# Forgetting attention of a two-group decoder step: another block order, one turning of the gate rows, other places for the chains at block ends

## The reference, cut to what matters

```
cum = jnp.cumsum(logf, axis=1)                      # one gate row per head
s = einsum('bqhe,bkhe->bhqk', q, k) * SCALE         # prompt: 2048 x 2048, causal
s = s + cum[query] - cum[key]
out = einsum('bhqk,bkhe->bqhe', softmax(s), v)
```

## Time and profile before

| | |
|---|---|
| three runs | 3190.3, 3173.29, 3172.47 us (median 3173.29) |
| the profiled execution's own time | 3176.38 us |
| its span | 3174.6 us |
| PE, DVE, ACT, POOL busy in the span | 93%, 51%, 31%, 24% |
| granted TensorE clock, mean of the span | 0.97 |

### The profile page before, as it was taken

One profiled execution on the slowest core, in us unless ns is written; L12 is line 12 of the kernel. 1 busy time (PEld: TensorE's weight loads), 2 busy tenths in 40 slices (PEclk: granted clock), 3 DMA queues, 4 the chain that ended last, 5 costly groups with the idle time before them and its releaser, 6 DMA issues. The chain is left out here.

```text
span 3174.6 us, 44387 instructions
## 1 busy us (share of the span) xinstructions
PE 2963.3 (93%) x15753; PEld 2460.9 (78%) x15753; DVE 1629.9 (51%) x3067; ACT 976.5 (31%) x2022; POOL 747.1 (24%) x510
## 2 busy tenths in 40 slices
PE   8999999878877899979979999999999999999998
PEld 6888889744344499967769999999998788888886
DVE  5113210367677688865745555554556544444445
ACT  4223221355555455543232221112214111111112
POOL 4002100123433254532101122211121221122210
PEclk9999999888999899989989999999999999999999
DMA  4465336456665334337653111112113411111101
GB/s 155 157 212 175 112 130 177 145 151 197 174 185 164 95 112 113 97 95 243 197 195 138 40 40 40 40 43 77 40 47 109 151 53 40 40 40 60 59 13 54
DMA packets 237238, 349.80 MB, mean 110 GB/s; under 512 B 75321, under 2 KB 172122, under 8 KB 231119
## 3 DMA queue, kind: packets, MB, share of 16 engines
q1 hardware_dynamic: 236151, 325.40, 32.7%
q0 software_dynamic: 944, 22.61, 1.9%
HBM read 283.14 MB, written 93.97 MB: 119 GB/s over the span
## 5 line engine op out<-in xcount | busy, mean ns | idle before, releaser
L2706 POOL TENSOR_TENSOR cm_dn_lo<-cm_dn_raw,cm_dn_hi 128x1024 fp32r<-128x1024 f32 x44 | 108.3, 2482 | 974.4 <-ACT cm_dn_hi L2755 974.4
L3443 PE MATMUL pj_acc<-pj_w_hi,pj_h_hi 128*128 128x480 f32 (+3 forms) x896 | 335.1, 374 | 0.9 <-DVE pj_h_lo L3318 0.9
L3444 PE MATMUL pj_acc<-pj_w_lo,pj_h_hi 128*128 128x480 f32 (+3 forms) x896 | 333.5, 372 | 0.0
L3445 PE MATMUL pj_acc<-pj_w_hi,pj_h_lo 128*128 128x480 f32 (+3 forms) x896 | 333.3, 372 | 0.0
L2999 PE MATMUL cm_g_ps<-cm_h_hi,cm_up_hi 128*128 128x344 f32 (+1 forms) x880 | 310.4, 353 | 12.0 <-DVE cm_h_lo L2811 10.9
L3001 PE MATMUL cm_g_ps<-cm_h_hi,cm_up_lo 128*128 128x344 f32 (+1 forms) x880 | 309.0, 351 | 0.0
L2999 PE MATMUL cm_u_ps<-cm_h_hi,cm_up_hi 128*128 128x344 f32 (+1 forms) x880 | 308.2, 350 | 0.0
L3000 PE MATMUL cm_g_ps<-cm_h_lo,cm_up_hi 128*128 128x344 f32 (+1 forms) x880 | 308.2, 350 | 0.0
L3001 PE MATMUL cm_u_ps<-cm_h_hi,cm_up_lo 128*128 128x344 f32 (+1 forms) x880 | 307.8, 350 | 0.0
L3000 PE MATMUL cm_u_ps<-cm_h_lo,cm_up_hi 128*128 128x344 f32 (+1 forms) x880 | 307.0, 349 | 0.0
L3324 DVE TENSOR_TENSOR pj_w_lo<-area,pj_w_hi 128x480 fp32r<-128x480 f32 (+3 forms) x112 | 75.6, 698 | 381.2 <-ACT pj_w_hi L3280 381.1
(11 more groups left out here) (459 smaller groups left out, 6557.7 us busy)
## 6 DMA issues: line engine op xcount, KB each, us to landing
area<-in_w_up SPq DMA_DIRECT2D x44, 1024.0 KB, 6.8
fp_kv_low<-in_fox_kv SPq DMA_DIRECT2D x168, 256.0 KB, 2.9
area<-in_fox_kv SPq DMA_DIRECT2D x88, 256.0 KB, 2.9
cm_dn_raw<-in_w_down SPq DMA_DIRECT2D x44, 512.0 KB, 3.6
out_s_win<-in_cache POOLq DMA_DIRECT2D x8, 2047.0 KB, 9.2
proj_a<-area SPq DMA_DIRECT2D x48, 240.0 KB
sp_raw<-proj_b SPq DMA_DIRECT2D x16, 640.0 KB, 4.2
area<-in_w_a SPq DMA_DIRECT2D x10, 960.0 KB, 7.0
```

The costliest lines, as they stand in the source:

```text
L2706: pool.tensor_tensor(dn_lo[:, s], dn_raw[:, s], dn_hi[:, s].bitcast(F32), ALU.subtract).then_inc(dn_ready, 1)
L3443: pe.matmul(out, h_hi[:, k, place(t)], w_hi[:, j % 2, k, 0:wide], start=(k == 0), stop=False)
L3444: pe.matmul(out, h_hi[:, k, place(t)], w_lo[:, j % 2, k, 0:wide], start=False, stop=False)
L3445: last = pe.matmul(out, h_lo[:, k, place(t)], w_hi[:, j % 2, k, 0:wide], start=False, stop=(k == KT - 1))
```

## The change

- **Order of blocks.** Heads 1 and 3 take their blocks in falling order, so the blocks have 4, 8, 12, 16, 16, 12, 8, 4, 4, 8, 12, 16, 16, 12, 8, 4 slots. The scores of the next block are spread evenly over 3 or 4, 7, 10 or 14 slots of a block of 4, 8, 12 or 16.
- **Gate rows.** `k_aug` keeps the rows of all heads side by side, so one turning gives 16 rows; the gate parts are 4 and no longer 16. POOL copies them once to the second half of `k_more`. `m_tok` and the rows of `q_more` have 16 rows too, zero outside the head's own four.
- **Places.** Query parts come in slot 1, keys in slots listed in `keys_at`. At a block's end PE does `turn_max` and then the block's last `value` (the other way round after blocks of 4 slots); `copy_o` comes ahead of the next block's first `exp`.
- **Output.** The turning of the output is a matmul with `fold`, two unit matrices one above the other, which adds the halves; `normalise` is one instruction, from one buffer `o_tok`. Blocks of 4 slots get one more small matmul, with zeros, that clears a corner of `o_ps`.
- **Sample.** `attend` does the 16 pages of a part in its slot 15, the four groups are fetched again from slot 16 on, the result is kept at slot 17, and `product` is two POOL instructions of half the size.
- **Start.** The fill of `q_more` goes from POOL to DVE in the projection; the first scores come after four of the first six parts.

```diff
-    blocks = [(h, q) for h in range(H) for q in range(4)]
+    blocks = [(h, q if h % 2 == 0 else 3 - q) for h in range(H) for q in range(4)]
...
+    scores_at = {}
+    for b in range(NBLK - 1):
+        within = {4: 4 if size[b + 1] == 8 else 3, 8: 7, 12: 10, 16: 14}[size[b]]
+        for n in range(size[b + 1]):
+            scores_at.setdefault((b, n * within // size[b + 1]), []).append(n)
+
+    keys_at = {(0, 3): (0, 2), (1, 5): (0, 3),
+               (2, 5): (1, 0), (2, 7): (1, 1), (2, 9): (1, 2), (3, 5): (1, 3),
+               (5, 5): (2, 0), (5, 7): (2, 1), (5, 9): (2, 2), (6, 5): (2, 3),
+               (9, 5): (3, 0), (10, 5): (3, 1), (10, 7): (3, 2), (10, 9): (3, 3)}
+    parts_at = {at: [("k", *part)] for at, part in keys_at.items()}
+    parts_at[0, 0], parts_at[1, 6] = [("a", 2)], [("a", 3)]
+    for b in range(NBLK - 2):
+        parts_at[b, 1] = [("q", b + 2)]
...
-                            fetched < RING or part_slot((fetched - RING) // QUARTS, 16 + (fetched - RING) % QUARTS) <= slot):
+                            fetched < RING or part_slot((fetched - RING) // QUARTS, 16) <= slot):
...
-                pool.tensor_tensor(prod[:, n % 2], quarter(n)[:, :, 0],
-                                   q_own[:, a // 2:a // 2 + 1].to_broadcast([P, QUART, F]), ALU.mult
-                                   ).then_inc(multiplied, 1)
+                for pair in (slice(0, 2), slice(2, 4)):
+                    last = pool.tensor_tensor(prod[:, n % 2, pair], quarter(n)[:, pair, 0],
+                                              q_own[:, a // 2:a // 2 + 1].to_broadcast([P, 2, F]), ALU.mult)
+                last.then_inc(multiplied, 1)
...
-                    if at == 20:
+                    if at == 17:
                         keep(a)
...
-                    if at in range(15, 15 + QUARTS):
-                        attend(a, at - 15)
+                    if at == 15:
+                        for k in range(QUARTS):
+                            attend(a, k)
...
+                    if b == 2 and i == 0:
+                        pool.wait_ge(part_hi, part_no["a", 3])
+                        pool.tensor_copy(k_more[0:AUGS, 1], k_more[0:AUGS, 0].bitcast(F32)).then_inc(aug_spread, 1)
...
             def normalise(b):
...
-                dve.link(v, v.tensor_copy(o[:, j:], z[:, j:, 0]))
-                v.tensor_tensor(o[:, j:], o[:, j:], z[:, j:, 1], ALU.add).then_inc(o_joined, 1)
-                v.wait_ge(o_joined, b + 1)
-                v.tensor_tensor(o, o, rden[:, b % 2].unsqueeze(2).to_broadcast([P, 4, HD]),
-                                ALU.mult).then_inc(o_ready, 1)
+                if b >= 1:
+                    v.wait_ge(stored[(b - 1) % 2], 16 * ((b - 1) // 2 + 1))
+                v.tensor_tensor(o_tok[:], z_ps[:, 0:4 * HD].rearrange("p (j e) -> p j e", e=HD),
+                                rden[:, b % 2].unsqueeze(2).to_broadcast([P, 4, HD]), ALU.mult).then_inc(o_ready, 1)
...
-                    if i == 2 and b > 0:
+                    if i == 0 and b > 0:
                         copy_o(b - 1)
...
+                    if q == 0 and i == 1:
+                        pe.wait_ge(k_zeroed, 3)
+                        pe.matmul(o_ps[HD:P, 0:P], nothing[:], probs[:, u % PROBS, 0:P], start=True, stop=True)
...
-                    last = pe.transpose(z_ps[:, j * P:(j + 1) * P], oT[:, j * P:(j + 1) * P], ident)
+                    last = pe.matmul(z_ps[:, j * HD:(j + 1) * HD], oT[:, j * P:(j + 1) * P], fold[:], start=True, stop=True)
...
-                    if i == 1 and b > 0:
-                        value(b - 1, size[b - 1] // GROUP - 1)
...
-                if b + 1 < NBLK:
+                if b + 1 < NBLK and size[b] > 4:
                     turn_max(b + 1)
-            value(NBLK - 1, size[NBLK - 1] // GROUP - 1)
+                value(b, size[b] // GROUP - 1)
+                if b + 1 < NBLK and size[b] == 4:
+                    turn_max(b + 1)
```

171 lines of the change are left out of this document (89 added, 82 removed).

## The result

The changed kernel takes 3160.79 us (median of 5 runs, 3154.71 to 3161.12), the kernel before 3180.58 us (median of 5 runs beside them, 3172.47 to 3190.3). The ratio is 0.9935, with a 95% interval of 0.9909 to 0.996: 0.65% faster, some 20 us. The forecast was 3118 us, 55 us less than before; the range began above at 3158. The direction was right, the size a third of what was forecast.

A forecast was written before the change was run, and what follows sets the result against it. The prediction saw a 478.6 us stage with PE standing 108 us, mainly for ACT's score buffers. Terms summed to −54.9 us: 3176.4 became 3121.5, adjusted to 3118 for the runs' median; range 3080 to 3158.

The forecast's parts named there:

- burst and hops: Sample: four `attend` groups at once outlast the two score buffers, +6 us; hops over DVE and PE come closer, +5 us.
- block ends: At block ends, PE's waits for the query split, maxima and row copies all go: −22.2 us, between −25 and −11.
- the edges: Stage start and end: earlier scores without waiting for POOL's fill, −1.5 us; fewer DVE instructions before the last sums, −2.2 us.
- Gate rows: 12 of 16 gate parts go: −7.8 us of PE work and −5.0 us of waits ahead of them.
- taken at the same: Output: `turn_o` as a matmul with `fold` could cost 6 to 23 us; taken as unchanged from 11.5, nothing gained.
- Spreading: Scores spread over slots: one-score slots take 2.05 us, within 1.93 to 2.35; −25.4 us, between −36 and 0.
- third rival: Sample's chain on PE: uncovered bursts and hops cost 6.5 us per part, 104 us in all; 3212 us, chance 0.09.
- Split product: POOL's sample `product` in halves: DVE stands behind POOL half as long, −3 us, between 0 and −8.
- first rival: Dense round stays the bound: one-score slots cost 2.35 us, half of block-end waits return; 3155 us, chance 0.20.
- fourth rival: On SP, a store behind the 16 page issues makes `normalise` hold up DVE: +28 us, 3146 us, chance 0.08.
- second rival: All PE waits in the stage go and the granted clock rises: −97 us, 3076 us, chance 0.13.
- signs given for right and wrong: Right: one-score slots at 2.0 to 2.1 us; wrong: 2.3 us, DVE store waits, or PE waits at 634, 637 or burst.

The follow-up runs named there:

- w1: Changed kernel with rising block order, scores two to a slot as before and key parts in scoreless slots of 16-slot blocks: 3177.06 us, ratio 0.9998 to before.
- v2: Block order, score spreading and key places undone as in w1, plus `attend` and fetches spread and `keep` at slot 20: 3163.05 us, 0.9951 to before.
- x1: Changed kernel with `attend` spread over slots 15 to 18, pages fetched one by one, result kept at slot 20: 3143.89 us, 0.9888 to before.
- v1: Kernel before with only the change's block ends; artefact: its query load kept its old place and came late, 19.1 us. 3204.11 us, 1.0077 to before.
- y2: Changed kernel with `turn_max`, last `value` and `copy_o` in the old order, query parts still in slot 1: 3177.5 us, 0.9989 to before.
- z3: Changed kernel with query parts, and the next head's query load, back to two slots before a block's end: 3168.14 us, 0.9966 to before.
- y3: Changed kernel with the output turned by transposes and its halves joined on DVE as before: 3161.15 us, 0.9938 to before.
- z1: Changed kernel without the 12 key parts and key loads of heads 1 to 3: 3126.64 us, 0.9851 to before.
- z2: Kernel before without the key parts and key loads of heads 1 to 3: 3162.39 us, 0.9956 to before.
- w2: Kernel before with only POOL's `product` split into two half-size instructions: 3173.06 us, 0.9994 to before.
- y4: Changed kernel with `attend` spread as in x1 and key parts moved off `value` slots as in x2: 3134.83 us, 0.9877 to before.
- x4: Changed kernel with scores packed two to a slot from slot 0 of each block: 3194.91 us, 1.0045 to before.
- y1: Changed kernel with every head's blocks in rising order and key parts set anew: 3199.69 us, 1.0056 to before.
- x3: Changed kernel with POOL's `product` as one whole instruction again: 3176.51 us, 0.9985 to before.
- x2: Changed kernel with key parts moved one slot later, off slots with a `value`: 3154.6 us, 0.992 to before.

## Why the prediction was wrong

The direction was right, the size was not: its −55 us were −20. By three pieces, each measured one with about 9 us of uncertainty:

| piece | forecast | measured |
|---|---|---|
| order, spreading, keys (w1 to changed, v2 to x1) | −25 | −20 |
| burst and hops (changed to x1, w1 to v2) | +11 | +15 |
| all the rest (v2) | −40.5 | −16 |
| sum | −55 | −21 |

Most of what is missing lies in the last piece. In v2's stage the terms of that piece forecast 33.9 us less standing of PE (22.2 at block ends, 5.0 at gate parts, 3.0 for the product, 3.7 at the edges) and 6.6 us less work; measured were 12.5 and 0.6 us.

**Block ends: the step that failed.** "All of 13.5 + 5.0 + 3.7 = 22.2 us goes" was read off the list of waits as if each named wait stood by itself. Some of what was named did go: of the 13.5 us for the query's split 0.8 are left, at line 940. But in the changed kernel `turn_max` still stands 14.6 us: 6.6 for the split of a key part and 8.0 for the maxima. Three of the four waits for a key part are at the ends of blocks of 12 slots, where the change puts one in slot 9. With order, scores and key parts as before, in v2, `turn_max` stands only 3.8 us, and what went turns up elsewhere: 7.0 us at `part` and 2.3 at `turn_o`, where query and key parts follow each other through the one bank, and 7.5 us more at `score` (59.5 for 52.0). In v1 `score` stands 11.4 us more. A query part in slot 1 puts two copies on ACT and a split on DVE where the next block's scores begin. The forecast asked what is late next for the last `value` only, not for the place to which the part was moved. All the same y2 and z3, 17 and 10 us slower, show that in the changed kernel the new places are the better ones; its slot 1 has two scores in 6 blocks of 14, that of w1 in 11. What the term is worth by itself is not shown: v1 has the artefact. That it is the copies in slot 1 that delay the scores is read from the lists; no kernel moved them alone onto an engine that is free.

**Gate rows.** The busy part was right: 7.5 us of PE fell away for 7.8 forecast. In v2's stage PE's busy time is unchanged all the same: the gate parts cost 1.2 us there, but the folding matmul 21.3 for 11.5 and the zeros 2.5. `turn_o` had been taken at the same although its upper bound was 11.5 us more; in the changed kernel it came out in the middle. Together with DVE's 15 us, booked at nothing, it makes no difference in time that y3 could show: two errors that cancel, which is luck.

**Spreading.** The one-score slot was taken at 2.05 us. A block of 16 slots with 12 such slots and 4 without scores would by the forecast take 12 × 2.05 + 4 × 1.47 = 30.5 us; the one at 757.94 took 29.39, at a granted clock of 1.00. But it is the best of the four. Its twin at 978.51 took 35.09, and 4.9 of the 5.7 us between them are PE's busy time at a granted clock of 0.85. For the blocks at 936.38 and 715.28 the forecast's values give 2 × 3.22 + 12 × 2.05 + 2 × 1.47 = 34.0 us, and they took 42.13 and 42.66 (715.28 to 757.94); two bursts each lie in them, and granted clocks of 0.84 and 0.92. The forecast's 129 us for the four were 149. So 2.05 us holds for one block at full clock; by the same sum the other three have one-score slots of 2.4 to 2.8 us. The 20 us that the bundle is worth contain, by the medians of z1 and z2, about 13 us lost to key parts. Moving them from slots where ACT and DVE had nothing to do to slots where they hold up a score was a moved step for which the sum had no term.

**The burst.** The place was named and the mechanism was right: it outlasts the two buffers and ACT and DVE run dry. Size: 15 us, with the 11 booked inside its uncertainty; the third rival's 104 us were far off. 0.9 us a part is far below the 4.1 us from which that rival would have decided.

**Split product.** The rule cited in the forecast, from the Trainium skill, SBUF — State Buffer, Who interferes with whom, would make the gain nil if the second half follows at once. The halves do follow at once, and this is what DVE does beside such a pair (changed kernel, POOL and DVE in order of time):

```profile
954.05 2.50 POOL L469 TENSOR_TENSOR fp_prod<-fp_kv_low,fp_q_own 128x512 f32<-128x512 f32 x2 [2.85 <-DVE fp_s_dec L514]
...
954.48 0.87 DVE L547 TENSOR_SCALAR fp_p_row<-fp_extra,sp_consts 8x4 f32<-8x4 f32 x1
955.27 0.20 DVE L549 TENSOR_REDUCE fp_den_dec<-fp_p_dec 128x4 f32<-128x64 f32 x1
955.50 1.06 DVE L550 TENSOR_TENSOR fp_den_dec<-fp_den_dec,fp_extra 1x4 f32<-1x4 f32 x1
```

DVE's first instruction ends at 955.35, where the first half ends (954.05 + 1.25 = 955.30), and the third at 956.56, where the second does (956.55). So DVE gets its turn between the halves: the rule's exclusion is seen here, and issue order gives the gap to DVE. It does not always: a cast on DVE that starts at 636.67 takes 2.50 us, through both halves. DVE's busy time falls by 10 and 24 us. The size on the path, −3 us, can't be told from what w2 measured in the kernel before, −2 us with 7 to either side. In the changed kernel it is −16, and without the split DVE is stretched more: 325.0 us busy, where 314.4 less the 13 us of the two instructions of `normalise` would be about 301, with 44 stretched instructions for 25. Why there are more collisions in the changed order was not tried.

**The rivals.** The first rival's 3155 us lies near the 3161 measured, but that is luck. Its main condition, that spreading is worth nothing, goes against the bundle's 20 us, found twice. Its other one, that half of the block-end waits come back, fits the size (14.6 of 22.2 us are left), but only 8.0 of them are maxima. DVE waits for no store in the lists; the fourth rival had no part in it. The time ahead of the stage stayed as it was. The clock did not rise (0.91 before and after), so the second rival failed at its condition; y4, with 25 us less standing, has 0.94.

**The signs given for right and wrong.** "Wrong if the stage's PE waits turn up at lines 634, 637 or the burst" has happened: 634 from 5.4 to 17.0 us. One-score slots of 2.0 us have happened in one block of four, and those of 2.3 and more in the other three.

Open: why undoing single parts costs 10 to 38 us each while the whole rest is worth 16 and the bundle 20. For x4 the key parts are a reason that was not tried by itself; y1, y2, z3 and x3 have only the general one that each place was chosen with the others in it. And how much of each difference is the clock, below.

## What to carry to other kernels

A wait that goes from the list is not a gain until it is said who next uses that engine, bank or slot: price every moved step at its new place, by the engines that it occupies there, not only at the old one. Ask of each long piece on the busiest engine whether it is longer than the buffers that feed the others; if so, spread it, as `attend` over four slots here, 15 us. To price a bundle, undo all of it together and each piece against two backgrounds: single undoings here added up to several times the whole.

## What the runs showed of the hardware

PE's busy time for the same work is not fixed. y4 and x4 have the same number of PE instructions in the stage (2054 and 2055 records) and are busy 351.2 and 384.4 us, at granted clocks of 0.94 and 0.86; PE stands still 83 us in one and 114 us in the other. So from y4 to x4 31 us of standing go with 33 us of longer work; which brings which, no run separates. Nor do the two go in step over the kernels of the table: x4 and the changed kernel both stand 23% of the stage, at 0.86 and 0.91, x2 and v2 both 21%, at 0.90 and 0.92. The twin blocks of the changed kernel show it within one run: 26.3 us busy at 1.00, 31.2 us at 0.85. From the kernel before to the changed one neither the standing nor the clock moved. The Trainium skill, TensorE: Matmul & The Clock Gate, Part 1, calls throttled the default which activity releases; y4 and x4 agree with it in direction, the table as a whole not closely.

Two POOL instructions back to back mostly let DVE in between: in the changed kernel only two of about 50 stretched DVE instructions run longer than 1.35 us. Cutting one POOL product in two took 10 to 24 us off DVE's busy time over 64 products, cutting it in four another 12. It does not hold for every pair: in v1 a cast of 128x4 on DVE took 7.28 us beside POOL instructions of 4.50 and 2.34 us that followed each other.
